# A delta rule without the products that nobody reads: 24 fillers taken from each pair of heads

## The chip, the cores and the metric

One core of a Trainium2 chip runs the whole kernel. The metric is the device time of one execution in microseconds. The engines are TensorE (PE in the profile; its weight loads are PEld), VectorE (DVE), ScalarE (ACT), GpSimd (POOL) and SyncE (SP). TensorE's granted clock is shown in the profile as a share of its full 2.4 GHz; the two levels are 1.00 (2.4 GHz) and 0.50 (1.2 GHz).

## The reference, cut to what matters

The reference is two blocks of two layers each on a sequence of 512 tokens with 1024 features. The first block's two layers each mix tokens by a convolution, a differential attention and a gated delta rule on 6 heads of 64, run forwards and backwards, and then apply a feed-forward network. The second block has a layer with a recurrent time mix (RWKV) and one with sparse attention and a mixture of experts. The change lies in the delta rule of the first block:

```python
kb = kc * bc[..., None]
A = jnp.where(strict, jnp.einsum("bhncd,bhnsd->bhncs", kb, kc) * decay, 0.0)
rhs = jnp.concatenate([vc * bc[..., None], kb * jnp.exp(gc)[..., None]], axis=-1)
sol = lax.linalg.triangular_solve(A, rhs, left_side=True, lower=True, unit_diagonal=True)
u, w = sol[..., :Dv], sol[..., Dv:]
Aqk = jnp.einsum("bhncd,bhnsd->bhncs", qc, kc) * decay
...
def step(state, inp):
    u_i, w_i, qg_i, aqk_i, kdec_i, gl_i = inp
    v_new = u_i - jnp.einsum("bhcd,bhde->bhce", w_i, state)
    o = jnp.einsum("bhcd,bhde->bhce", qg_i, state) + jnp.einsum("bhcs,bhse->bhce", aqk_i, v_new)
    state = state * gl_i[..., None, None] + jnp.einsum("bhcd,bhce->bhde", kdec_i, v_new)
    return state, o
```

## The kernel before

The kernel is written engine by engine: each phase is a block in which every engine has its own list of instructions, and the lists meet at counting semaphores (`wait_ge`, `then_inc`) inside the phase and at a barrier of all engines at its end. An engine works through its list strictly in order, so an instruction that waits holds up everything behind it on that engine.

`first_block` loops over two layers. In each, `delta_net` first makes the decays and normalised inputs (`delta_inputs`) and then loops over 3 pairs of heads. One pair goes through three phases, with 4 streams (2 directions by 2 heads) and 4 chunks of 128 tokens in each:

- `delta_prepare`: ScalarE stages k, q and v (L1440), TensorE multiplies k by k and q by k for each head (L1461, operands on 64 rows) and transposes k and v (L1468). VectorE builds the decay matrices (L1408), multiplies them by the products (L1421), and last multiplies the seen matrices (L1426); ScalarE takes exponentials (L1444) and GpSimd adds the identity (L1434).
- `invert`: the triangular matrices of the 4 streams are inverted by 7 levels of doubling. For each of the 28 items TensorE does 4 transposes (L1567) and 4 products (L1580, in the last level L1583), which the profile counts as 8 instructions; VectorE masks the transposes (L1548), and ScalarE takes the products (L1533) and makes the scan's inputs beside them. The same `invert` is called by the second block's time mix, once for each of its two groups of heads, behind `rwkv_prepare` and ahead of `rwkv_scan`; neither of these is changed. Of them, `rwkv_prepare` has no filler at its end, and `rwkv_scan` has 4 fillers ahead of its first step and none between its steps.
- `delta_scan`: TensorE first applies the inverses (L1661, L1669: "the solve"), ScalarE copies the results out (L1711, L1713). Then come 4 steps; in each, for both directions, TensorE passes the state on (L1683), VectorE subtracts (L1632), TensorE forms the state's growth (L1693) and the outputs (L1702, L1703), VectorE updates the state (L1645), and ScalarE copies the outputs (L1718).

`fill_in` (L235 to L239) is the filler: n products of a constant 128x128 tile with 512 columns, written to a PSUM bank whose contents nobody reads. Each is one instruction of 512 columns. In the delta rule it stands at the end of TensorE's list in the preparation (14 of them), between the solve and the scan's first step (4), and in each of steps 1 to 3 of the scan once for each direction, behind the wait for the state (6 in all):

```python
pe.wait_ge(state_ready[d], s)
fill_in(nc, mem, mem.bank[4 + d], 1)
pe.wait_ge(fresh_ready[d], 2 * s)
```

Other phases of the kernel have fillers too; they stay.

Of the kernel before, what the change touches and what calls it, by code (L numbers as in the profile page):

```python
# [234 lines left out]
def fill_in(nc, mem, bank, n):  # L235

    tile = mem.filler[:, :]
    for _ in range(n):
        nc.tensor.matmul(bank[:, :], tile, tile.unsqueeze(1).broadcast_to([P, SEQ // P, P]), start=True, stop=True)  # L239
# [1143 lines left out]
def delta_prepare(nc, mem, u, cols, rows, hp, b):  # L1383


    with buffers(nc, v=[P, SEQ]) as (v,), phase(
# [65 lines left out]
        @block.tensor  # L1452
        def _(pe):
            pe.wait_ge(staged, 1)
            for n in range(4):
                if n == 2:
                    pe.wait_ge(staged, 2)
                lanes = slice((n % 2) * HEAD, (n % 2 + 1) * HEAD)
                for t in range(TT):
                    right = (b.k if n < 2 else b.q)[lanes, t * P:(t + 1) * P]  # L1460
                    last = nc.tensor.matmul(mem.bank[4 + n][:, t * P:(t + 1) * P], b.k[lanes, t * P:(t + 1) * P],  # L1461
                                            right, start=True, stop=True)
                last.then_inc(product, 1)
                if n < 2:

                    pe.wait_ge(staged, 2 * n + 1)
                    for t in range(TT):
                        last = nc.tensor.transpose(mem.bank[2 + n][:, t * P:(t + 1) * P],  # L1468
                                                   (b.k, v)[n][:, t * P:(t + 1) * P], CONST(mem.const, "ident"))
                    last.then_inc(turned, 1)  # L1470
            fill_in(nc, mem, mem.bank[0], 14)


class ScanInputs:
# [124 lines left out]
def delta_scan(nc, mem, y, hp, b):  # L1599

    first_tile = CONV_T + PAIRS1
    with buffers(nc, w=[P, 2, SEQ], state=[P, 2, HEAD], fresh=[P, 2, 2, P], o=[P, 2, SEQ]) as (
# [50 lines left out]
        @block.tensor  # L1653
        def _(pe):
            for d in range(2):
                for par in range(2):
                    n = 2 * d + par
                    for t in range(TT):
                        c = slice(t * P, (t + 1) * P)

                        last = nc.tensor.matmul(mem.bank[d][:, t * P + par * HEAD:t * P + (par + 1) * HEAD],  # L1661
                                                b.twice[:, n, c], vb[:, n, t, :], start=True, stop=True)
                last.then_inc(solved, 1)
                for par in range(2):
                    n = 2 * d + par
                    for t in range(TT):
                        c = slice(t * P, (t + 1) * P)

                        last = nc.tensor.matmul(mem.bank[2 + d][lanes[par], c], kb[:, n, t, :], b.twice[:, n, c],  # L1669
                                                start=True, stop=True)  # L1670
                last.then_inc(solved, 1)
            fill_in(nc, mem, mem.bank[4], 4)
            pe.wait_ge(solved_taken, 4)
            for s in range(TT):
                for d in range(2):
                    if s == 0:
                        continue
                    t = chunk[d](s)
                    pe.wait_ge(state_ready[d], s)
                    fill_in(nc, mem, mem.bank[4 + d], 1)  # L1680
                    pe.wait_ge(fresh_ready[d], 2 * s)
                    for par in range(2):
                        nc.tensor.matmul(mem.bank[d + 2 * par][:, 0:HEAD], w[lanes[par], d, t * P:(t + 1) * P],  # L1683
                                         state[lanes[par], d, :], start=True, stop=True).then_inc(passed[d], 1)
                for d in range(2):
                    t = chunk[d](s)
                    c = slice(t * P, (t + 1) * P)
                    pe.wait_ge(fresh_ready[d], 2 * s + 2)
                    if s >= 1:
                        pe.wait_ge(state_ready[d], s)  # L1690
                    for par in range(2):
                        n = 2 * d + par
                        last = nc.tensor.matmul(mem.bank[4 + d][lanes[par], 0:HEAD], kd[:, n, t, :],  # L1693
                                                fresh[:, d, s % 2, par * HEAD:(par + 1) * HEAD], start=True, stop=True)
                    last.then_inc(grown[d], 1)
                    if s >= 1:
                        pe.wait_ge(out_taken[d], s)
                    for par in range(2):
                        n = 2 * d + par
                        to = mem.bank[6 + d][lanes[par], 0:P]  # L1700
                        if s >= 1:
                            nc.tensor.matmul(to, state[lanes[par], d, :], qg[lanes[par], d, c], start=True, stop=False)  # L1702
                        last = nc.tensor.matmul(to, fresh[:, d, s % 2, par * HEAD:(par + 1) * HEAD], b.seen[:, n, c],  # L1703
                                                start=(s == 0), stop=True)
                    last.then_inc(out_ready[d], 1)
# [1964 lines left out]
```

## Time and profile before

| What | Value |
|---|---|
| three timed runs | 4149.51, 4169.4, 4170.1 us (median 4169.4) |
| the profiled execution: its time, its span | 4155.43 us, 4153.6 us |
| instructions | 54607 |
| TensorE busy | 3861.2 us (93%) |
| TensorE weight loads | 3250.6 us (78%) |
| VectorE, ScalarE, GpSimd busy | 1556.6, 1298.5, 290.5 us |
| mean granted TensorE clock | 0.947 |

The profiled execution is one run of its own; the instruction times in the rows come from it, and the span is the time from its first to its last instruction. Busy shares are means over very different stages. A TensorE that is busy may be so with fillers, and the ends of its products are modelled, so the start of one product and the start of the next are the better measure of how long one holds the engine.

### The profile page before, as it was taken

The numbers are of one execution on the slowest core, as the hardware profiler recorded it, in microseconds if no ns is written. First come the engines' busy times: TensorE is split into PE (matmuls) and PEld (weight loads), VectorE is DVE, ScalarE is ACT, GpSimd is POOL, SyncE is SP. The second block draws the span as 40 slices with busy tenths as digits, with TensorE's granted clock in tenths as the row PEclk, the third lists the DMA queues.
The fourth block names the chain that finished last, engine by engine and source line by source line (L and its number), as shares of the span: only waits on it lengthen the run. The fifth ranks groups of instructions, "written<-read, shape, count | busy, mean of one in ns | idle before, by whom it ended". The sixth has DMA issues, their size and how long they took to land. (4 is left out here: it accounts for less than half of the span.)

```text
span 4153.6 us, 54607 instructions
## 1 busy us (share of the span) xinstructions
PE 3861.2 (93%) x21239; PEld 3250.6 (78%) x21239; DVE 1556.6 (37%) x2723; ACT 1298.5 (31%) x2324; POOL 290.5 (7%) x220
## 2 busy tenths in 40 slices
PE   8999999999999899999997889999998879999998
PEld 7778876787877787678775777877876659999997
DVE  3575535232457553423245554323336430000001
ACT  3475434231247453423132333322213311111111
POOL 0351000000025100000000000000000000000000
PEclk9999989999999898999998989999999789999999
DMA  4000012221300001222121001222321025665664
GB/s 146 29 1 1 0 41 82 97 84 61 99 35 1 1 0 41 77 95 91 61 92 36 1 1 71 95 93 76 108 67 67 10 101 193 233 236 202 228 231 136
DMA packets 64063, 344.83 MB, mean 83 GB/s; under 512 B 9116, under 2 KB 15132, under 8 KB 33452
## 3 DMA queue, kind: packets, MB, share of 16 engines
q1 hardware_dynamic: 59020, 330.59, 22.6%
q0 software_dynamic: 4896, 12.27, 1.5%
q8 instruction: 95, 1.56, 0.2%
q14 instruction: 52, 0.43, 0.0%
HBM read 328.27 MB, written 13.50 MB: 82 GB/s over the span
## 5 line engine op out<-in xcount | busy, mean ns | idle before, releaser
L511 PE MATMUL bank<-high 128*128 128x512 f32 x2480 | 973.2, 392 | 39.3 <-DVEq L619 22.8
L512 PE MATMUL bank<-low,high 128*128 128x512 f32 x2480 | 971.2, 392 | 0.0
L513 PE MATMUL bank<-high,low 128*128 128x512 f32 x2480 | 970.7, 391 | 0.0
L511 PEld LDWEIGHTS bank<-high 128*128 128x128 f32 x2480 | 469.5, 189 | 143.7 <-DVEq L619 25.7
L513 PEld LDWEIGHTS bank<-high,low 128*128 128x128 f32 x2480 | 469.3, 189 | 98.1
L512 PEld LDWEIGHTS bank<-low,high 128*128 128x128 f32 x2480 | 469.4, 189 | 97.5
L535 ACT ACTIVATE high<-weight_ring 128x2048 fp32r<-128x2048 f32 (+1 forms) x148 | 274.7, 1857 | 571.0 <-PE bank L513 530.2
L585 DVE TENSOR_TENSOR low<-weight_ring,high 128x2048 fp32r<-128x2048 f32 (+1 forms) x148 | 328.5, 2220 | 325.7 <-ACT high L535 325.7
L3306 PE MATMUL bank<-chosen,glu_ring 128*128 128x176 f32 x2816 | 426.3, 314 | 2.8 <-ACT chosen L3370 2.8
L3306 PEld LDWEIGHTS bank<-chosen,glu_ring 128*128 128x128 f32 x2816 | 422.3, 191 | 4.8 <-issue 4.8
L239 PE MATMUL bank<-filler 128*128 128x512 f32 x971 | 291.5, 439 | 53.3 <-PEq L172 41.3
L239 PEld LDWEIGHTS bank<-filler 128*128 128x128 f32 x971 | 193.1, 206 | 109.2 <-issue 62.7
L3320 PE MATMUL bank<-hidden,down_ring 128*128 128x176 f32 x1408 | 211.3, 313 | 0.0
L3320 PEld LDWEIGHTS bank<-hidden,down_ring 128*128 128x128 f32 x1408 | 210.4, 190 | 0.0
L1548 DVE TENSOR_TENSOR joint<-bank,level_masks 128x512 f32<-128x512 f32 x224 | 153.9, 691 | 146.4 <-PE bank L1567 146.4
L891 POOL TENSOR_TENSOR y<-y,scaled 128x512 f32<-128x512 f32 x120 | 171.9, 1468 | 309.3 <-ACT scaled L926 308.6
L3428 DVE TENSOR_TENSOR hidden<-silu,bank 128x176 f32<-128x176 f32 x88 | 29.8, 338 | 390.0 <-ACT silu L3386 390.0
L593 DVE TENSOR_TENSOR gated<-gated,bank 128x512 f32<-128x512 f32 x86 | 59.0, 686 | 284.7 <-ACT gated L542 158.4
L742 POOL TENSOR_TENSOR h_branch<-x_res 128x512 f32<-128x512 f32 x16 | 16.1, 1039 | 2010.7 <-POOLq L172 2010.7
L663 DVE TENSOR_TENSOR u<-bank,scale 128x512 f32 (+1 forms) x84 | 58.1, 692 | 261.0 <-PE bank L513 261.0
L1580 PE MATMUL bank<-weight_ring,joint 128*128 128x128 f32 x1152 | 151.8, 276 | 0.0
L3386 ACT ACTIVATE silu<-bank 128x176 f32<-128x176 f32 x88 | 27.9, 318 | 391.6 <-PE bank L3306 391.6
(525 smaller groups left out, 4548.9 us busy)
## 6 DMA issues: line engine op xcount, KB each, us to landing
glu_ring<-in_w_expert SPq DMA_DIRECT2D x88, 1024.0 KB, 6.8
weight_ring<-in_w_ff SPq DMA_DIRECT2D x64, 1024.0 KB, 4.9
down_ring<-in_w_expert_down SPq DMA_DIRECT2D x64, 704.0 KB, 5.1
weight_ring<-in_w_in SPq DMA_DIRECT2D x22, 1024.0 KB, 4.8
weight_ring<-in_w_ffe SPq DMA_DIRECT2D x22, 1024.0 KB, 4.9
weight_ring<-in_w_downe SPq DMA_DIRECT2D x16, 704.0 KB, 4.1
weight_ring<-in_w_ino SPq DMA_DIRECT2D x11, 1024.0 KB, 4.8
weight_ring<-in_w_ine SPq DMA_DIRECT2D x9, 1024.0 KB, 4.9
```

The source lines that it names most:

```text
L239: nc.tensor.matmul(bank[:, :], tile, tile.unsqueeze(1).broadcast_to([P, SEQ // P, P]), start=True, stop=True)
L511: nc.tensor.matmul(mem.bank[b][:, :], whole, high[:, k, :], start=(k == 0), stop=False)
L512: nc.tensor.matmul(mem.bank[b][:, :], whole, low[:, k, :], start=False, stop=False)
L513: last = nc.tensor.matmul(mem.bank[b][:, :], rest, high[:, k, :], start=False, stop=(k == kt - 1))
L535: nc.scalar.activation(w_high[:, s, :], mem.ring[:, s, 0:size], ACT.Copy).then_inc(high_ready[s], 1)
L585: nc.vector.tensor_tensor(w_low[:, s, :], mem.ring[:, s, 0:size], w_high[:, s, :], ALU.subtract).then_inc(low_ready[s], 1)
L593: nc.vector.tensor_tensor(whole, whole, mem.bank[b][:, :], ALU.mult).then_inc(taken[b], 1)
L891: nc.gpsimd.tensor_tensor(y[:, c, :], y[:, c, :], scaled[:, n % CONV_SLOTS, :], ALU.add).then_inc(added, 1)
L1548: nc.vector.tensor_tensor(chunks(joint[:, n, :]), chunks(turn_bank(i)[:, :]), mask, ALU.mult) \
L1580: last = nc.tensor.matmul(product_bank(i)[:, c], joint[:, n, c], matrix[:, n, c], start=True, stop=True)
L3306: last = nc.tensor.matmul(two(low[s])[:, half, :], glu_ring[:, s, at:at + P], chosen[:, k, :], start=(k == 0), stop=(k == KD - 1))
L3320: last = nc.tensor.matmul(two(high[m // 2])[:, m % 2, :], down_ring[:, s, k * P:(k + 1) * P], hidden[:, k, :], start=(k == 0), stop=(k == ...
```

## The change

The three calls of `fill_in` in the delta rule's preparation and scan go: 14, 4 and 6 products for each pair of heads. Nothing else is added, moved or changed; what the kernel computes is the same.

```diff
@@ -1468,7 +1468,6 @@
                         last = nc.tensor.transpose(mem.bank[2 + n][:, t * P:(t + 1) * P],
                                                    (b.k, v)[n][:, t * P:(t + 1) * P], CONST(mem.const, "ident"))
                     last.then_inc(turned, 1)
-            fill_in(nc, mem, mem.bank[0], 14)
 
 
 class ScanInputs:
@@ -1669,7 +1668,6 @@
                         last = nc.tensor.matmul(mem.bank[2 + d][lanes[par], c], kb[:, n, t, :], b.twice[:, n, c],
                                                 start=True, stop=True)
                 last.then_inc(solved, 1)
-            fill_in(nc, mem, mem.bank[4], 4)
             pe.wait_ge(solved_taken, 4)
             for s in range(TT):
                 for d in range(2):
@@ -1677,7 +1675,6 @@
                         continue
                     t = chunk[d](s)
                     pe.wait_ge(state_ready[d], s)
-                    fill_in(nc, mem, mem.bank[4 + d], 1)
                     pe.wait_ge(fresh_ready[d], 2 * s)
                     for par in range(2):
                         nc.tensor.matmul(mem.bank[d + 2 * par][:, 0:HEAD], w[lanes[par], d, t * P:(t + 1) * P],
```

## Rows read from the trace of the kernel before

**Rows 1.** The page: span, and the filler's group (busy us, mean ns, idle before).

```profile
span 4153.6 us, 54607 instructions
...
L239 PE MATMUL bank<-filler 128*128 128x512 f32 x971 | 291.5, 439 | 53.3 <-PEq L172 41.3
```

**Rows 2.** Timeline of TensorE, first pair: start us, us, instruction [idle before <- releaser].

```profile
306.29 4.30 PE L239 MATMUL bank<-filler 128*128 128x512 f32 x14
313.28 1.50 PE L1567 MATMUL bank<-const_cols,weight_ring 128*128 128x128 f32 x12 [2.69 <-PEq L172]
...
316.12 1.95 PE L1580 MATMUL bank<-weight_ring,joint 128*128 128x128 f32 x16
...
353.20 1.97 PE L1661 MATMUL bank<-more,h_branch 128*128 128x64 f32 x16 [1.50 <-PEq L172]
```

**Rows 3.** Timeline: VectorE's last work of the preparation, pairs one and three.

```profile
309.84 2.48 DVE L1426 TENSOR_TENSOR weight_ring<-bank,weight_ring 128x512 f32<-128x512 f32 x4
...
474.21 5.56 PE L239 MATMUL bank<-filler 128*128 128x512 f32 x14
...
477.56 2.48 DVE L1426 TENSOR_TENSOR weight_ring<-bank,weight_ring 128x512 f32<-128x512 f32 x4
```

**Rows 4.** Windows: length, busy PE, PEld, DVE, ACT, POOL, granted clock, DMA share, GB/s.

```profile
304.00:306.00 2.00, 2.00 (x15) 2.00 (x13) 2.00 (x9) 1.70 (x4) 0.00 (x0) 0.50 0.00 0
306.00:309.00 3.00, 3.00 (x10) 2.29 (x10) 3.00 (x13) 0.45 (x1) 2.10 (x2) 0.66 0.00 0
317.00:323.00 6.00, 6.00 (x56) 6.00 (x55) 2.56 (x5) 5.63 (x13) 2.56 (x2) 1.00 0.01 1
362.00:376.00 14.00, 14.00 (x103) 8.36 (x99) 3.46 (x17) 1.84 (x7) 0.00 (x0) 1.00 0.00 1
2307.00:2311.00 4.00, 4.00 (x21) 4.00 (x20) 2.08 (x3) 0.00 (x0) 0.00 (x0) 0.50 0.01 2
2311.00:2312.00 1.00, 1.00 (x8) 1.00 (x7) 0.09 (x1) 0.60 (x1) 0.00 (x0) 0.66 0.00 0
2372.00:2376.00 4.00, 3.44 (x37) 2.47 (x36) 0.56 (x3) 0.66 (x3) 0.00 (x0) 1.00 0.00 0
```

**Rows 5.** Timeline of TensorE, start of the inversion in the second block's time mix.

```profile
2306.59 2.79 PE L1567 MATMUL bank<-const_cols,neg 128*128 128x128 f32 x12 [4.63 <-PEq L172]
...
2311.71 1.95 PE L1580 MATMUL bank<-neg,joint 128*128 128x128 f32 x16
```

**Rows 6.** Timeline of all engines, first pair's scan, its start, second step and end.

```profile
360.05 1.19 PE L239 MATMUL bank<-filler 128*128 128x512 f32 x4
...
360.65 0.59 ACT L1713 ACTIVATE w<-bank 128x512 f32<-128x512 f32 x1
...
361.29 0.34 PE L1693 MATMUL bank<-fresh,more 128*64 128x64 f32 x4
...
366.98 0.49 PE L239 MATMUL bank<-filler 128*128 128x512 f32 x1
...
367.20 0.28 DVE L1645 SCALAR_TENSOR_TENSOR state<-state,last_decay,bank 128x64 f32<-128x64 f32 x1 [1.28 <-PE bank L1703]
...
367.41 0.44 PE L1683 MATMUL bank<-state,w 64*128 64x64 f32 x4
...
367.95 0.35 DVE L1632 TENSOR_TENSOR fresh<-more,bank 128x64 f32<-128x64 f32 x2 [0.47 <-PE bank L1683]
...
368.20 0.44 PE L1683 MATMUL bank<-state,w 64*128 64x64 f32 x4
368.57 0.34 PE L1693 MATMUL bank<-fresh,more 128*64 128x64 f32 x4
...
376.33 0.43 PE L1703 MATMUL bank<-weight_ring,fresh 128*64 128x128 f32 x2
```

**Rows 7.** Timeline of TensorE, the fourth pair's solve, from its start to the fillers.

```profile
1400.47 3.64 PE L1661 MATMUL bank<-more,h_branch 128*128 128x64 f32 x16 [1.50 <-PEq L172]
...
1410.42 1.20 PE L239 MATMUL bank<-filler 128*128 128x512 f32 x4
```

## The prediction, made before the changed kernel was run

> **What bounds the kernel now.** I read the page first, then the timeline of one pair of heads in the delta rule, engine by engine, and last the granted clock of short stretches in it. The page gives a span of 4153.6 us and, among TensorE's work, the filler product at L239, whose result nobody reads: 971 of them, 291.5 us [rows 1]. Busy time of that kind says nothing of the bound, so each stage has to be read for the wait that ends last. The change takes 24 fillers from each pair of heads, and the loops run 3 pairs in 2 layers: 6 x 24 = 144 of the 971.
>
> In the preparation TensorE's last product is out when the fillers begin at 306.29; they end at 310.59, but VectorE works on until 309.84 + 2.48 = 312.32, and only then does the inversion start, at 313.28 [rows 2, 3]. VectorE bounds this phase. In the inversion TensorE is busy for all of 6 us while VectorE is for 2.56 [rows 4]: TensorE bounds it, for 38.4 us (313.28 to 353.20 less the pause of 1.50) [rows 2]. In the scan TensorE is busy for all of 14 us, fillers included [rows 4].
>
> The second thing to see is the clock. From 304 to 306 TensorE is busy throughout and yet granted 0.50, the level of 1.2 GHz. From 306 to 309 the mean is 0.66: at two levels, 0.50 and 1.00, that is (1.00 - 0.66) x 2 x 3 = 2.0 us of the low one, so it came up to 2.4 GHz at about 308.0, within the fillers, and the inversion runs at 1.00 [rows 4]. The preparation's own products do not lift the clock; the fillers do.
>
> **Preparation, 14 fillers (L1471).** They lie beside VectorE in all six pairs. In the first they end 1.73 us before it does; the closest case is the third, 474.21 + 5.56 = 479.77 against 477.56 + 2.48 = 480.04 [rows 2, 3]. They are on no path: gain 0. With VectorE's cover gone it would be up to 4.3 us a pair. What is late next is the clock: without them TensorE is idle for 7 us, from 306.3 to 313.28, and enters the inversion, which it bounds, at 0.50. The trace has that very case. The second block's time mix calls the same inversion with nothing ahead of it. It starts at 2306.59, is at 0.50 from 2307 to 2311, and comes up within 2311 to 2312 [rows 4, 5], after 12 transposes, 8 product instructions and 4 transposes. To the start of the next run of 16 product instructions that took 2311.71 - 2306.59 = 5.12 us; the warm one takes 316.12 - 313.28 = 2.84 [rows 2, 5]. The loss is 2.28 us; a second start of this kind, 103 us later in the same block, went alike. Nothing later absorbs it, as TensorE has no gap behind it: 6 x 2.28 = +13.7 us. The bounds: the clock comes up as early as under the fillers, 308.0 - 306.29 = 1.7 us after dense work begins, which at the same ratio, (5.12 - 2.84)/5.12 = 0.45, costs 0.8; or as late as in the fourth pair's solve, dense from 1400.47, which took 9.95 us to 1410.42 where the first pair's took 360.05 - 353.20 = 6.85, so 3.1 [rows 2, 6, 7]. That is +5 to +19 in all.
>
> The Trainium skill speaks against a quick recovery here. "TensorE: Matmul & The Clock Gate", in its part on PE-mode transpose, says that the full clock is not engaged for transposes as it is for other products. Of the inversion's instructions a third are transposes, the first 12 among them. By that rule alone the low level could last much longer (the second rival below); the row has the rise after some 5 us, and the sum goes by the row.
>
> **Between solve and scan, 4 fillers (L1672).** They run 360.05 to 361.24; the next product starts at 361.29, released by ScalarE's copy of w, which ends at 360.65 + 0.59 = 361.24 [rows 6]. ScalarE is the cover, gain 0; without it, 1.2 us a pair. TensorE is idle here for 1.2 us instead. That could let the clock fall: the pause of 1.50 us before the solve [rows 2] did so in four of the six pairs. This one is shorter and has dense work on both sides, so I take no fall and keep it as the first rival.
>
> **Scan, 6 fillers (L1680), one for each direction in steps 1 to 3.** TensorE has no gap here, so they do cost. In step 2 the first starts at 366.98, direction 0's products (L1683) at 367.41, and after a second filler direction 1's at 368.20, then L1693 at 368.57 [rows 6]. Without fillers direction 0's products start at 366.98. VectorE's subtraction L1632 followed them by 367.95 - 367.41 = 0.54 and lasts 0.35, so it runs from 367.52 to 367.87, just behind the state update L1645, which ends at 367.20 + 0.28 = 367.48 [rows 6]. Direction 1's products wait for that update: 367.48 plus 0.06 for the signal is 367.54 (an estimate, by the 0.05 between ScalarE's end and the product at 361.29), and they hold the engine 0.37 (368.20 to 368.57), to 367.91. L1693 waits for L1632 too: 367.87 + 0.06 = 367.93. It stood at 368.57, so 0.64 us of the two fillers' 0.86 is gained, and the state update is what is late next. Three such steps make 1.92, six pairs -11.5 us. Bounds: all six fillers at 0.43 make 2.58 a pair (-15.5); one of the two in each step makes 1.29 (-7.7).
>
> **The solve, touched only in when it comes.** It takes 6.85 us with the clock up; in three pairs it took 1.6 more and in the fourth 3.1 [rows 7], 7.9 in all, by when the pause ahead of it came. The change shifts that. I take it unchanged; the ends are -7.9 and 6 x 3.1 - 7.9 = +10.7.
>
> **Sum.** 0 + 13.7 + 0 - 11.5 + 0 = +2.2 us. What looks like 144 instructions saved is a trade of nearly equal sizes. The profiled execution took 4155.43 us around its span of 4153.6; it becomes 4157.6. The three timed runs are 4149.51, 4169.4 and 4170.1, so their median lies 14 above the profiled one and the runs differ by 20. The middle of all four, (4155.43 + 4169.4)/2 = 4162.4, plus 2.2 is my forecast: 4165. About 0.5%, 21 us, is what a measurement of this kernel can tell from no change.
>
> **Rivals.**
> First, the clock falls at the scan's start or in it (slower), because its fillers hold it. For it: the preparation's products on 64 rows, a kind that the scan has too (L1683, L1702), kept TensorE busy at 0.50 without lifting it [rows 4], so a scan once low would stay low to its end. Against it: the second block's scan has no fillers between its steps and was granted 1.00 even in 4 us with TensorE busy for 3.44 [rows 4]. Price: the scan runs from 361.29 to 376.76, 15.5 us, less 1.9 [rows 6]; at the inversion's ratio 5.12/2.84 = 1.8 that would be +10.9 a pair, and as its waits on VectorE don't stretch I take 9.5. All six: 4165 + 57 = 4222. It decides from three pairs on (28 us).
>
> Second, the inversion stays at 0.50 throughout (slower). 38.4 us at 1.8 times is +30.7 a pair in place of 2.3; six make +170, so 4335. Against it: both starts of that kind came up [rows 5]. The skill's rule on transposes would lead here.
>
> Third, the fillers' own time is on the path after all (faster): 4.30 + 1.19 + 2.58 = 8.1 us a pair, 48 in all, no clock lost, 4114. Against it stand VectorE's end at 312.32 and ScalarE's at 361.24 [rows 3, 6].
>
> Fourth, the inversions lose only 0.8 each and the scan gains its full 2.58: 4.8 - 15.5 = -10.7 us, 4152, inside no change.
>
> **How the numbers follow.** Forecast with the fourth case and the solve's ends in it: 0.80. Scan cold in all or half of the pairs: 0.10. Inversion cold: 0.03. Fillers on the path: 0.04. Other shifts of the clock, either way: 0.03. The range is the runs' own 4149.5 to 4170.1 widened by the terms' ends, -10.7 - 2.2 = -13 to bring 4137, and +18.6 - 7.7 = +11 to bring 4181; I take 4140, and 4188 above to let in one or two cold scans. Faster by over 0.5% has 0.06, within it 0.80, slower 0.14.
>
> **What would show it.** Right: TensorE idle some 7 us before each inversion, 0.50 at the inversion's start and 1.00 within 7 us of it; VectorE's L1426 ending as before; the scan 1.9 us shorter with 1.00 throughout. Wrong: 0.50 inside a scan, an inversion at 0.50 beyond 7 us, a scan shortened by less than 1.3, or a preparation shortened at all.

## The result and the profile after

The changed kernel takes 4188.25 us (median of 10, 4177.65 to 4219.52) against 4163.1 us before (median of 10, 4149.51 to 4170.1): ratio 1.0069, 95% interval 1.0046 to 1.0093. (The ratios here are taken over all runs of a kernel and differ a little from those of the medians, 1.0060 in this case.) It is slower by 25 us where +2.2 was forecast, and it lies just outside the range (4188).

The page of the changed kernel, the lines that answer to [rows 1]; 144 fillers are gone and TensorE's busy time fell by 2 us only, since what is left runs slower:

```profile
span 4186.6 us, 54355 instructions
...
PE 3859.1 (92%) x21095; PEld 3251.3 (78%) x21095; DVE 1556.0 (37%) x2723; ACT 1297.7 (31%) x2324; POOL 288.9 (7%) x220
...
L239 PE MATMUL bank<-filler 128*128 128x512 f32 x827 | 239.5, 432 | 53.1 <-PEq L172 41.7
```

The first pair's timeline, where the fillers of the preparation stood ([rows 2, 3]): VectorE's last work ends at 316.97 and the inversion starts 0.97 later, as before; TensorE has waited 6.96 us for it, and the first 12 transposes now hold it for some 2.6 us (the same run of the second pair, shown further down: 404.56 to 407.14) where they held it for 1.4. (Line numbers behind L1471 are smaller by 1 to 3 in the changed kernel.)

```profile
307.89 3.09 PE L1461 MATMUL bank<-q,k 64*128 64x128 f32 x16
...
314.50 2.47 DVE L1426 TENSOR_TENSOR weight_ring<-bank,weight_ring 128x512 f32<-128x512 f32 x4
...
317.94 2.80 PE L1566 MATMUL bank<-const_cols,weight_ring 128*128 128x128 f32 x12 [6.96 <-PEq L172]
```

Windows of the changed kernel (columns as in [rows 4]), the first pair from preparation to scan, then the second pair's solve, pause and scan, and the fourth pair's scan:

```profile
303.00:317.00 14.00, 7.98 (x37) 6.58 (x35) 13.98 (x49) 5.91 (x11) 4.94 (x4) 0.50 0.00 0
318.00:322.00 4.00, 4.00 (x19) 4.00 (x20) 2.08 (x3) 0.00 (x0) 0.00 (x0) 0.50 0.00 0
324.00:330.00 6.00, 6.00 (x57) 6.00 (x56) 2.60 (x4) 5.69 (x13) 2.55 (x2) 1.00 0.00 1
372.00:384.00 12.00, 11.57 (x100) 7.20 (x94) 3.38 (x18) 1.94 (x7) 0.00 (x0) 1.00 0.00 1
...
453.00:456.00 3.00, 3.00 (x31) 2.81 (x30) 0.30 (x2) 0.71 (x2) 0.00 (x0) 1.00 0.00 0
456.00:457.00 1.00, 0.12 (x2) 0.00 (x0) 0.00 (x0) 0.85 (x2) 0.00 (x0) 1.00 0.00 0
460.00:477.00 17.00, 17.00 (x80) 9.89 (x78) 2.54 (x12) 1.39 (x5) 0.00 (x0) 0.50 0.00 0
...
1432.00:1453.00 21.00, 20.99 (x110) 12.76 (x108) 3.68 (x18) 1.94 (x7) 0.00 (x0) 0.50 0.00 1
```

The reader should see two things. The first pair's scan is at 1.00 and does 100 products in 12 us. The second pair's scan has TensorE busy for all of 17 us and does only 80: it runs at 0.50. A column of busy time alone would call the second the better one.

The timeline of TensorE at that point, second pair, shows where it fell. Up to 459.25 instructions have the lengths of the warm scan (0.34, 0.43), from 459.61 they take 0.69 in place of 0.43:

```profile
454.54 1.58 PE L1668 MATMUL bank<-h_branch,more 128*64 128x128 f32 x16
457.29 0.34 PE L1690 MATMUL bank<-fresh,more 128*64 128x64 f32 x4 [1.18 <-ACT w L1710]
457.46 0.39 PE L1700 MATMUL bank<-weight_ring,fresh 128*64 128x128 f32 x4
...
458.11 0.66 PE L1680 MATMUL bank<-state,w 64*128 64x64 f32 x8
458.99 0.34 PE L1690 MATMUL bank<-fresh,more 128*64 128x64 f32 x4 [0.21 <-DVE fresh L1631]
459.25 0.43 PE L1699 MATMUL bank<-qg,state 64*64 64x128 f32 x2
459.61 0.69 PE L1700 MATMUL bank<-weight_ring,fresh 128*64 128x128 f32 x2
```

From such timelines each pair can be cut into four stretches by the first start of a product in each: the preparation, and behind it inversion (L1567 to L1661, with the pause), solve (L1661 to the scan's L1693, with the pause or the fillers between) and scan (to the end of its last L1703). The table has their lengths in us for pairs 1 to 6.

| kernel | inversion | solve | scan |
|---|---|---|---|
| before | 39.9 in each | 8.1, 9.7, 9.7, 11.2, 8.1, 9.7 | 15.5 in each |
| changed | 42.2, 41.6, 41.4, 42.4, 41.6, 41.4 | 11.3, 11.2, 8.1, 13.5, 11.2, 8.1 | 13.5, 20.4, 13.5, 21.8, 20.4, 13.5 |
| sums, before | 239.5 | 56.4 | 92.9 |
| sums, changed | 250.5 (+11.0) | 63.3 (+6.9) | 103.0 (+10.2) |

The preparation to the inversion's start is 15.8 to 15.9 us in both. So the delta rule lost 28.1 us in the profiled executions. Their spans differ by 33.0; another 4.7 stands ahead of the first pair (302.14 against 297.46), in code that is the same in both.

### The profile page after: what moved, and what is told of

It is laid out like the page before. It is cut to its first block and busy times, and to the rows that moved or that the text cites. A ratio compares the mean times of both kernels' runs of the same rounds, so it can differ in the third digit from the quotient of the medians.

```text
span 4186.6 us, 54355 instructions
## 1 busy us (share of the span) xinstructions
PE 3859.1 (92%) x21095; PEld 3251.3 (78%) x21095; DVE 1556.0 (37%) x2723; ACT 1297.7 (31%) x2324; POOL 288.9 (7%) x220
## 5 line engine op out<-in xcount | busy, mean ns | idle before, releaser
L239 PE MATMUL bank<-filler 128*128 128x512 f32 x827 | 239.5, 432 | 53.1 <-PEq L172 41.7
L239 PEld LDWEIGHTS bank<-filler 128*128 128x128 f32 x827 | 162.4, 204 | 96.2 <-issue 57.6
L663 DVE TENSOR_TENSOR u<-bank,scale 128x512 f32 (+1 forms) x84 | 58.1, 691 | 261.0 <-PE bank L513 261.0
```

## The experiments

The question was why three scans fell. Three theories stood at first: the pause of 1.2 us between solve and scan lets the clock fall (P); the scan's own work can't hold it (S); it is an effect of the cold inversion (I). The first four kernels take the change apart. In the edits `...` marks unchanged lines.

**e1: only the 14 go.**

```diff
-            fill_in(nc, mem, mem.bank[0], 14)
```

> Only the 14 fillers at the end of the preparation are left out; the 4 behind the solve and the 6 in the scan stay. Theory P (pause): the slow scans of the changed kernel come from the 1.24 us pause between solve and scan, so here every scan keeps 15.5 us at clock 1.00; what is lost is only the slow start of the six inversions, 1.4 to 2.5 us each, 11 in all, and what the solves make of the shifted moments (8 us either way). About +11 us, 4174. Theory S (scan's own fillers): the scan needs its 6 fillers, which it has here: the same, +11. Theory I (inversion): the missing 14 fillers are the cause of it all, since all that follows comes at another clock: +25 us or more, with slow scans among the six.

Measured: 4197.96 us (4 runs) against 4156.14, ratio 1.0088 (1.0054 to 1.0122). All six scans took 15.5 us at 1.00, as P and S say. The six inversions took 42.0 to 42.6, together +14.0. But the solves took 11.3, 11.3, 14.3, 11.3, 14.3 and 12.9, together 75.2, which is +18.8 and above what any theory had. All six fell. The longest stayed at 0.50 through its whole solve and came up under the 4 fillers (timeline of TensorE, third pair):

```profile
538.58 3.10 PE L1660 MATMUL bank<-more,h_branch 128*128 128x64 f32 x16 [1.49 <-PEq L172]
541.60 2.88 PE L1668 MATMUL bank<-h_branch,more 128*64 128x128 f32 x16
544.41 3.68 PE L1660 MATMUL bank<-more,h_branch 128*128 128x64 f32 x16
548.02 2.88 PE L1668 MATMUL bank<-h_branch,more 128*64 128x128 f32 x16
550.83 2.08 PE L239 MATMUL bank<-filler 128*128 128x512 f32 x4
552.84 0.34 PE L1692 MATMUL bank<-fresh,more 128*64 128x64 f32 x4
```

So these 4 fillers may have a second use that I had not seen: to take a cold solve's clock up before the scan begins. The third and the fifth solve of e1 were at 0.50 to their last product and came up in the stretch of the fillers (the other four came up before it). Where the 4 fillers are missing, five solves stayed at 0.50 to their end (one each in the changed kernel and e10, three in e9), and all five scans behind them ran at 0.50 throughout. No run changes this alone.

**e2: only the 4 between solve and scan go.**

```diff
-            fill_in(nc, mem, mem.bank[4], 4)
```

> Only the 4 fillers between the solve and the scan are left out. Theory P: the clock falls within 4 us of the scan's start in some of the six pairs (2 to 4), though the 14 and the 6 are there; whether the scan's fillers bring it back is open: between +2 us a pair (back within one step) and +8 (not before the end), so +5 to +30 us. Theory S: TensorE's pause there is too short to matter, all scans at 1.00 and 15.5 us, total unchanged within 5 us. Theory I: unchanged too.

Measured: 4169.67 us, ratio 1.0025 (1.0004 to 1.0046). In the profile all six scans took 15.5 us, the first with this window, though TensorE waited 1.17 us ahead of it:

```profile
369.00:384.00 15.00, 14.95 (x116) 9.16 (x116) 3.97 (x20) 1.94 (x8) 0.00 (x0) 1.00 0.00 1
```

In this execution P in its plain form fails: the pause with the scan's fillers behind it did not bring the clock down once in six. But the profiled execution, 4155.39 us at a mean granted clock of 0.947, is the second shortest of ten. Five of the others took 4171.6 to 4181.79 us at 0.939 to 0.942; of the 25 runs of the kernel before that were measured beside them one took more than 4170, and none was under 0.941. The median is 13.5 us above that of before, within what P expected (+5 to +30). So e2 doesn't show that the pause alone is harmless; where those executions lost their clock is open.

**e3: only the 6 in the scan go.**

```diff
                     pe.wait_ge(state_ready[d], s)
-                    fill_in(nc, mem, mem.bank[4 + d], 1)
                     pe.wait_ge(fresh_ready[d], 2 * s)
```

> Only the 6 fillers in the scan's steps are left out; the 14 and the 4 stay. Theory P: with no pause ahead of it the scan stays at 1.00 in all six pairs and takes 13.5 us in place of 15.5: -12 us, 4151, the solves as before (8 us either way). Theory S: the scan's own work can't hold the clock, so 1 to 4 of the six scans fall to 0.50 at some point and take 16 to 21 us: between -5 and +20 us. Theory I: -12 us as P.

Measured: 4153.17 us, ratio 0.9992 (0.9975 to 1.0009). All six scans took 13.5 us at 1.00 (first pair's below), so S falls: the scan's own work holds the clock if it starts without a pause. The solves took 58.1 together, +1.6 on before. The profiled span is 4142.1, 11.5 below that of before, as the 12 us of the scans would have it; but it is the shortest of ten, and the medians are 3 us apart.

```profile
366.00:379.00 13.00, 12.58 (x112) 7.88 (x106) 3.60 (x19) 1.94 (x7) 0.00 (x0) 1.00 0.00 1
```

**e4: the 4 and the 6 go, the 14 stay.**

```diff
-            fill_in(nc, mem, mem.bank[4], 4)
...
-                    fill_in(nc, mem, mem.bank[4 + d], 1)
```

> The 4 and the 6 are left out, the 14 at the end of the preparation stay: the changed kernel with warm starts of its inversions. Theories P and S: slow scans (20 to 22 us) in about half of the pairs, as in the changed kernel, and 13.5 us in the others; the inversions 39.9 us each. So the changed kernel less 11 us: 4177, +14 against before. Theory I: the clock holds, all scans 13.5 us, -12 us, 4151.

Measured: 4182.25 us, ratio 1.0045 (1.0024 to 1.0065). The inversions took 39.9 each and the scans 13.5, 20.3, 20.7, 20.8, 20.4 and 20.8: five of six fell. In the profiled executions neither part does it alone: without the 4 none of six fell (e2), without the 6 none of six (e3), without both five of six. The timed runs lean the same way (+0.25% and -0.08% for the parts, +0.45% for both), but their intervals don't tell the whole from the sum of the parts. (One of e4's ten timed runs took 4156.07 us, so their number of slow scans can hardly be five in each.) e4 also clears the inversion and the solve: the fourth pair's solve here was warm (8.1), and its scan still fell. The windows are its solve and first step, and its scan:

```profile
1416.00:1424.00 8.00, 6.83 (x68) 6.28 (x69) 0.44 (x4) 2.17 (x4) 0.00 (x0) 1.00 0.00 0
1424.00:1425.50 1.50, 1.36 (x24) 1.03 (x24) 0.93 (x7) 0.56 (x2) 0.00 (x0) 1.00 0.00 0
1427.00:1444.00 17.00, 17.00 (x80) 9.91 (x78) 2.53 (x12) 1.39 (x5) 0.00 (x0) 0.50 0.00 0
```

The theory was now A: the pause and a scan without fillers together let the clock fall, and a pause of 1.5 us ahead of the solve does the same to the solve.

**e5: the changed kernel with the 4 put back.**

```diff
-            fill_in(nc, mem, mem.bank[0], 14)
...
-                    fill_in(nc, mem, mem.bank[4 + d], 1)
```

> The changed kernel with one part undone: the 4 fillers between solve and scan are back, the 14 and the 6 stay out. Theory A (pause and sparse scan together): a scan without its 6 fillers holds the clock if it starts without the 1.24 us pause, and falls if it has the pause, so all six scans take 13.5 us at 1.00; the inversions still start slow (42.0 to 42.6 us in place of 39.9, +14 in all) and the solves with them (11 to 14 us each where they were 8 to 11, up to +19): -12 + 14 + 0 to 19, so 4158 to 4177, some 15 to 25 below the changed kernel. Theory B (the scans' fall comes with the cold solves ahead of them): slow scans of 20 us remain in 2 to 4 pairs, total as the changed kernel, 4188.

Measured: 4164.56 us against 4161.74, ratio 1.0014 (0.9998 to 1.003). Six scans of 13.5 us, inversions +11.3 together, solves 61.1 (+4.7). One of the three parts undone takes back most of the loss, as A says; four of its six solves fell and took 11.2 or 11.3, and the scans behind them were warm, so B falls.

**e6: the kernel before, with 5 fillers more at the end of each inversion.**

```diff
                 if i < lag:
                     turn(i + lag)
+                if i == steps - 1:
+                    fill_in(nc, mem, turn_bank(i + 1), 2)
                 clear(i)
...
+            fill_in(nc, mem, turn_bank(steps), 3)
```

> The kernel before, nothing left out, with 5 fillers more at the end of each inversion: 2 ahead of its last product, where TensorE waits 0.58 us for VectorE, and 3 behind it, beside VectorE's last work (the inversions of the second block's time mix get them too). Theory A: it is the pause of 1.5 us ahead of the solve that lets the clock fall, so with some 0.65 us of it and the 0.58 filled the solve takes 8.09 us to the scan's start in all or nearly all pairs: -8 us, 4148. Theory C (the solve's own form, products of 64 columns or 64 wide, can't hold the clock): solves of 9.7 and 11.3 us in three or four of the six pairs as before, total unchanged.

Measured: 4151.68 us against 4161.74, ratio 0.9979 (0.9962 to 0.9996). All six solves took 8.1 us, 7.8 less together. C falls. (`invert` has these fillers in the second block's time mix too; its two inversions start 103.0 us apart with and without them.)

**e7: the same, with the 6 fillers of the scan left out.**

> The kernel before with the 6 fillers of the scan left out, the 14 and the 4 kept, and 5 fillers more at the end of each inversion. Theory A: scans of 13.5 us at 1.00 in all pairs (-12) and solves of 8.09 us (-8): -20 us, 4136, the fastest of all. Theory C: solves as before, -12 us or less, 4144 to 4150.

Measured: 4137.26 us (5 runs) against 4161.74, ratio 0.9937 (0.9916 to 0.9958): the fastest, 24 us below the kernel before and some 50 below the changed one. Solves of 8.1 and scans of 13.5 us in all six pairs. The timeline of TensorE at the end of the first inversion shows how the fillers lie in the gaps, with the pause now 0.80 in place of 1.50, and the window holds the whole way from the inversion's start (316.80) to just short of the scan's end (378.28) at 1.00:

```profile
353.27 0.71 PE L239 MATMUL bank<-filler 128*128 128x512 f32 x2
354.10 1.13 PE L1583 MATMUL bank<-joint,weight_ring 128*128 128x128 f32 x8
354.98 0.94 PE L239 MATMUL bank<-filler 128*128 128x512 f32 x3
356.72 1.97 PE L1664 MATMUL bank<-more,h_branch 128*128 128x64 f32 x16 [0.80 <-PEq L172]
```

```profile
316.00:378.00 62.00, 59.80 (x520) 53.20 (x521) 25.86 (x54) 31.48 (x91) 2.56 (x2) 1.00 0.01 1
```

**e8: e6 without the 14.**

> The 14 fillers of the preparation left out, the 4 and the 6 kept, and 5 fillers more at the end of each inversion. Without those 5 this kernel took 42 us more than before, 14 of it in the inversions and 19 in the solves, all six of which fell. Theory A: the solves fell because each pause came at the same moment after the clock's rise in the inversion, and with the pause half filled they stay at 1.00, 8.09 us: +14 - 8 = +6 us, 4162. Theory C: the solves fall here as there, 75 us together, 4198.

Measured: 4168.64 us, ratio 1.0013 (1.0 to 1.0027). Inversions 42.0 to 42.2 (+13.3 together), solves 8.1 and scans 15.5 in all six. Against e1, which differs by the 5 fillers alone but was measured at another time, it is 29 us faster. Against e6, measured at the same time, the missing 14 fillers cost 17 us, 13.3 of it in the inversions.

**e9: the changed kernel with 2 fillers back, those of step 1.**

```diff
                     pe.wait_ge(state_ready[d], s)
+                    if s == 1:
+                        fill_in(nc, mem, mem.bank[4 + d], 1)
                     pe.wait_ge(fresh_ready[d], 2 * s)
```

> The changed kernel with 2 of the 24 fillers back: those of the scan's step 1, one for each direction. The 14, the 4 and those of steps 2 and 3 stay out. Theory A: in the changed kernel the clock fell some 2.3 us after the scan's start, so what counts is how little TensorE does between the end of the solve and the end of step 1; two fillers in step 1 hold the clock in most of the six scans, which then take 14.2 us: 20 us below the changed kernel, 4165 to 4175. Theory D: a scan needs fillers in each of its steps once it starts with a pause: scans fall later, in step 2 or 3, and take 16 to 19 us; total above 4180.

Measured: 4194.05 us (5 runs) against 4164.09, ratio 1.0069 (1.0046 to 1.0092), a miss for A's numbers and not what D says either. Three pairs had scans of 14.2 us, which kept 1.00. In the other three the solve was at 0.50 from 0.6 to 0.8 us behind its start to its end (13.4 to 13.5 us) and the scan after it as well, 23.3 us. The window is the third pair's, from 2 us into its solve to the end of its scan:

```profile
528.00:562.00 34.00, 32.83 (x166) 22.88 (x165) 4.28 (x22) 4.12 (x11) 0.00 (x0) 0.50 0.00 0
```

Those scans did not fall, they began low. With the 4 fillers gone nothing took the clock up, and two fillers among the scan's work didn't either; they only added to it (23.3 us against 21.8). Three warm starts are too few to say that step 1 is the place.

**e10: the changed kernel again.**

> The changed kernel once more, unedited, for a second profiled execution: between 1 and 5 of the six scans slow (20 to 22 us), the others 13.5; the total follows their number, about 7 us each; each inversion 41.3 to 42.6 us. A theory by which the slow scans belong to certain pairs would have the same three, the second, fourth and fifth.

One execution, 4187.18 us: scans of 13.5, 20.5, 13.5, 21.8, 20.4 and 13.5, solves of 11.3, 11.1, 8.1, 13.5, 11.2 and 8.1. The same three pairs as in the first profile, to 0.1 us. Two executions are few, but they suggest that the count I had left open (1 to 5) is not chance from run to run alone: what comes in one pair fixes the moment of the next. e9 bears this out. Its first pair is that of e10 with 0.7 us more in the scan, and its second solve took 8.1 us where that of e10 took 11.1. The changed kernel's longest runs (4202.76 and 4219.52 us, mean granted clock 0.927 and 0.921 against 0.931 in the profile) have more of the low clock than either profile; where is not shown.

**e11: the changed kernel with the 5 fillers at the inversion's end.**

> The changed kernel, with 5 fillers more at the end of each inversion (2 ahead of its last product, 3 behind it). Theory A: the solves stay at 1.00 and take 8.09 us with the pause behind them, in all six (-15 us against the changed kernel), but the pause between solve and scan is still there and the scans still fall, in about half of the pairs or more: 4165 to 4180. Theory B (the scans fall because of the cold solves): all scans 13.5 us, 4150.

Measured: 4168.47 us against 4164.09, ratio 1.0005 (0.9996 to 1.0015). All six solves took 8.1 us, and three scans still fell (20.5, 20.4, 20.8), each after a warm solve. A holds here, and B falls for good.

## Why the prediction was wrong

**Preparation: hidden, right.** It takes 15.8 to 15.9 us with and without the 14 fillers; VectorE's cover was complete.

**Inversion at the low level: right, to within 3 us.** Priced at 2.28 us a pair, 13.7 in all. The changed kernel lost 11.0, e1 14.0, e8 13.3. The clock came up in each of the 42 inversions that started low, within 2.7 to 6.0 us, so the second rival has no support here. The Trainium skill says in "TensorE: Matmul & The Clock Gate", in its part on PE-mode transpose, that the full clock does not engage for transposes. This case's traces don't agree: the run is one third transposes, and from 408.62 the transposes themselves go at the warm pace (0.60 for 4, 0.44 from their start to the next product's) (timeline of TensorE, changed kernel, second pair):

```profile
404.56 2.79 PE L1566 MATMUL bank<-const_cols,weight_ring 128*128 128x128 f32 x12 [6.72 <-PEq L172]
407.14 1.64 PE L1579 MATMUL bank<-weight_ring,joint 128*128 128x128 f32 x8
408.62 0.60 PE L1566 MATMUL bank<-const_cols,weight_ring 128*128 128x128 f32 x4
409.06 1.95 PE L1579 MATMUL bank<-weight_ring,joint 128*128 128x128 f32 x16
```

**Scan where it stays warm: right.** 1.92 us a pair forecast, 2.02 measured (15.47 to 13.45), 0.7 of it in step 1 (14.2 in e9, which has the fillers of that step alone, against 13.5), where VectorE's update is a plain copy.

**Between solve and scan, and the scan's clock: this is the step that failed.** I took no fall after the pause, though the longer one of 1.50 us ahead of the solve had let the clock fall in four of six pairs, because this one is shorter and has dense work on both sides; and none within the scan, because the second block's scan holds the clock without fillers between its steps [rows 4]. Each looked at one part alone, and the profiles of e2 and e3 have no slow scan in twelve. But the change removes both at once. Without its fillers the scan behind the pause is less dense (12.58 of 13 us busy in e3, where it was 14 of 14 [rows 4]), and the row that I leaned on for the scan was of one with 4 fillers ahead of it, and thus without the pause. That the pause is needed is shown: all 18 scans without fillers and without the pause (e3, e5, e7) kept 1.00. That the scan's fillers make the pause harmless rests on one execution of e2, as said there. Of the scans that began at 1.00 with the pause and without fillers, 12 of 22 fell, each 1.7 to 2.5 us after its start (2 of 5 in the changed kernel, 2 of 5 in e10, 5 of 6 in e4, 3 of 6 in e11), and one each in the changed kernel and e10 began low after a cold solve and stayed so. In the changed kernel's profile the three slow scans cost 22.3 us, which I had at 0; with -12.1 for the scans' fillers, +11.0 for the inversions and +6.9 for the solves that makes the 28.1.

This was the first rival, with a chance of 0.10. It was right that the clock can fall there, and that a scan once low stays low to its end. Its reason, that the scan's fillers hold the clock, is half of it: without the pause the scan does without them. That its point of decision ("from three pairs on, 28 us") so nearly meets three pairs and +25 us is in part luck, since its price was 9.5 a pair where 7.0 to 8.3 was measured, and the solves, which it left out, made up the rest.

**Solve: taken unchanged, +6.9.** This term was mis-sized as well. Its ends (-7.9 to +10.7) held it in the changed kernel, not in e1 (+18.8). The range was said to have these ends in it, but its upper end was made of the inversions' +18.6 and the scans' -7.7 alone; with the solves' +10.7 it would be 4192. (Its lower end takes off the forecast's 2.2 once too often, which changes nothing here.) With the 14 fillers in place the solves averaged 9.4 us over 24 (before, e2, e3, e4), without them 11.0 over 30 (changed, e1, e5, e9, e10), and with the pause half filled 8.1 in all 24 of e6, e7, e8 and e11. So the fillers of the preparation seem to reach past the inversion. In e1 the pause came 35.1 to 35.8 us after the clock's rise in all six pairs and the clock fell in all six. An inversion that starts low ties the moment of its pause to the moment of its rise more closely than one that starts high. The other traces agree: of the 30 solves without the 14 fillers, those that fell are the 22 whose pause began 35.1 to 36.3 us after the rise, and the eight at 36.4 to 36.9 kept 1.00; of the 24 with them, the 15 at 40.6 to 43.0 fell and the nine at 43.3 to 43.8 did not. Whether a solve fell thus went with the moment of its pause, and a few tenths of a microsecond could decide. That reading is argued from the rows, not shown by an edit of its own.

What stays open: why some solves come up after 3 us and others not in 13; the 3 us in e3's timed runs where its profile has 12 less in the scans; and what e2's longer runs hold.

## What to carry to other kernels

A product that nobody reads can be off the path, and yet leaving it out can cost time in the next stage that TensorE bounds. Fillers that each look superfluous may stand in for one another, so take them out one place at a time and together, and read the granted clock of each stretch beside the busy share. Here the fillers between waits that TensorE has anyway (5 at the inversion's end) gained 10 us, and those in a stretch without gaps could go once no pause stood ahead of it. When a row is used to say that a stage will hold, check that it has the same stage ahead of it.

## What was not expected of the hardware

TensorE can be busy for 20.99 of 21 us at a granted clock of 0.50 without coming up (the fourth scan above), while at the end of a solve that had been dense and low for 12 us it came up in the stretch of 4 fillers of 512 columns (e1, two cases of two). A scan at the low level takes 20.3 to 21.8 us against 13.45, 1.5 to 1.6 times, less than the 1.8 of the inversion's first stretch (5.12 against 2.84 us); the one of 21.8 was low throughout, so a warm start doesn't explain it, and no run shows the cause. And the pattern of falls was the same in two executions: the same three pairs, with lengths within 0.1 us.
